# Issuing each step's up-row gathers as two groups of four, the second behind the next step's down-row gathers

## What is computed

```python
qv = (xb @ w_query).reshape(PEER_BLOCK, PEER_HEADS, 2, PEER_DHALF)
s = jnp.einsum('thsd,hskd->thsk', qv, keys)
sv, si = lax.top_k(s, PEER_TOPK)
...
g = jax.nn.softmax(fv, axis=-1)
u = expert_down[eidx]
act = jax.nn.gelu(jnp.einsum('thkd,td->thk', u, xb), approximate=False) * g
v = expert_up[eidx]
return jnp.einsum('thk,thkd->td', act, v)
```

## Time and profile before

| | us |
|---|---|
| median of 3 runs | 2114.09 (2113.5 to 2115.13) |
| the profiled execution | 2112.95 |
| its span | 2111.2 |
| PE, DVE, ACT, POOL busy | 1247.8, 1376.3, 431.7, 1052.5 |
| mean granted clock of TensorE | 0.779 |

### The profile page before, as it was taken

One profiled execution on the slowest core, in us unless ns is written; L12 is line 12 of the kernel. 1 busy time (PEld: TensorE's weight loads), 2 busy tenths in 40 slices (PEclk: granted clock), 3 DMA queues, 4 the chain that ended last, 5 costly groups with the idle time before them and its releaser, 6 DMA issues.

```text
span 2111.2 us, 20935 instructions
## 1 busy us (share of the span) xinstructions
PE 1247.8 (59%) x6676; PEld 741.8 (35%) x6676; DVE 1376.3 (65%) x3357; ACT 431.7 (20%) x920; POOL 1052.5 (50%) x1103
## 2 busy tenths in 40 slices
PE   5989899566568677777455848833224333332234
PEld 3855567453456445444223425510000000000000
DVE  3669971482477655577876676666776777777631
ACT  4112442621133221233210022211010110110000
POOL 1012220000336565566766566567767777777754
PEclk9889999687788888878778879976666665656655
DMA  9145671636669999999999999999989999999986
GB/s 297 56 159 183 204 266 55 218 100 231 227 250 373 398 402 398 394 405 396 404 404 395 402 375 398 399 386 410 409 323 409 385 409 410 410 409 409 409 341 278
DMA packets 260328, 696.11 MB, mean 330 GB/s; under 512 B 23743, under 2 KB 109847, under 8 KB 259119
## 3 DMA queue, kind: packets, MB, share of 16 engines
q0 software_dynamic: 149760, 545.33, 65.5%
q1 hardware_dynamic: 109346, 148.91, 21.0%
q10 hardware_dynamic: 1112, 0.53, 0.1%
HBM read 685.74 MB, written 9.08 MB: 329 GB/s over the span
## 4 chain that ended last, share of the span: by engine, by line
DMA 27%; POOL 17%; DVE 12%; issue 10%; PE 7%; DVEq 1%; ACT 1%; POOLq 0%; ACTq 0%
DMA arena<-in_expert_up_dram,rows 15%; DMA arena<-in_expert_down_dram,expert 11%; POOL arena L1894 9%; POOL arena L1914 8%; DVE arena L2572 6%; PE ps L2233 4%; PE ps L2265 2%; DVEq L2513 1%; DVE arena L2619 1%; PE ps L2444 1%; DMA arena<-in_expert_down_dram,sample 1%; DVE arena L2520 0%; DVE arena L2519 0%; DVE keys L2518 0%; DVE arena L2548 0%
## 5 line engine op out<-in xcount | busy, mean ns | idle before, releaser
L2572 DVE CUSTOM_DVE_ANT_0 arena<-arena,ps 128x1024 f32<-128x1024 f32 x512 | 611.5, 1218 | 283.3 <-DMA arena<-in_expert_down_dram,expert 273.0
L2233 PE MATMUL ps<-arena 128*32 128x512 f32 x2048 | 370.1, 858 | 641.5 <-DMA arena<-in_expert_up_dram,rows 641.5
L1914 POOL DMA_INDIRECT arena<-in_expert_up_dram,rows x512 | 487.3, 952 | 315.7 <-PE ps L2233 149.5
L1894 POOL DMA_INDIRECT arena<-in_expert_down_dram,expert x512 | 489.7, 956 | 231.9 <-issue 143.7
L2233 PEld LDWEIGHTS ps<-arena 128*32 128x32 f32 x2048 | 75.9, 137 | 868.2 <-issue 868.0
L2265 PE MATMUL ps<-arena 128*128 128x264 f32 (+1 forms) x1344 | 327.0, 402 | 39.6 <-ACT arena L1973 28.9
L2265 PEld LDWEIGHTS ps<-arena 128*128 128x128 f32 x1344 | 264.0, 200 | 110.8 <-ACT arena L1973 30.6
L720 PE MATMUL ps<-arena 128*128 128x256 f32 (+1 forms) x640 | 156.4, 400 | 3.5 <-ACT arena L549 3.5
L720 PEld LDWEIGHTS ps<-arena 128*128 128x128 f32 x640 | 123.6, 198 | 40.6 <-issue 19.9
L1934 ACT ACTIVATE arena<-arena 128x8 f32<-128x8 f32 x65 | 13.5, 208 | 588.5 <-DVE arena L2572 588.4
L467 POOL TENSOR_TENSOR arena<-arena 128x512 f32<-128x512 f32 x16 | 20.5, 1284 | 220.5 <-DVE arena L1073 220.5
(11 more groups left out here) (461 smaller groups left out, 1789.1 us busy)
## 6 DMA issues: line engine op xcount, KB each, us to landing
arena<-in_w_in_dram SPq DMA_DIRECT2D x42, 1024.0 KB, 17.4
arena<-in_w_ada_dram SPq DMA_DIRECT2D x32, 512.0 KB, 5.9
arena<-in_w_query_dram SPq DMA_DIRECT2D x16, 1024.0 KB, 17.2
arena<-in_w_ada_dram SPq DMA_DIRECT2D x8, 1024.0 KB, 17.5
arena<-in_w_ada_final_dram SPq DMA_DIRECT2D x16, 512.0 KB, 4.9
arena<-in_w_out_dram SPq DMA_DIRECT2D x8, 1024.0 KB, 19.3
arena<-in_expert_down_dram,expert POOLq DMA_INDIRECT x512, 12.3
arena<-in_expert_up_dram,rows POOLq DMA_INDIRECT x512, 12.3
```

The lines of the kernel that those rows point to most:

```text
L1894: G.indirect_dma_start(U[i], None, down, bass.IndirectOffsetOnAxis(ap=at, axis=0))\
L1914: G.indirect_dma_start(Vr[r][j], None, up, bass.IndirectOffsetOnAxis(ap=at, axis=0))\
L2233: last = mm(ps[32 * j:32 * j + 32, c, :], Z[:, j, m, :], Vr[r][4 * half + j][:, c * 512:(c + 1) * 512], start=(p % 4 == 0 and m == 0), sto ...
L2572: V.tensor_tensor_reduce(U[i], U[i], row, 1.0, 0.0, ALU.mult, ALU.add, dots[n % 2][:, j:j + 1]).then_inc(s_uused, 1)
```

## The change

Each step's eight up gathers are issued in two groups of four. The loop over the steps now issues: down of step n, the last four of up step n-5, the first four of up step n-4. Before it issued: down of step n, all eight of up step n-4. The gathers are the same, their buffers, semaphores and waits too; only their order in POOL's queue differs. PE's, DVE's, ACT's and SP's programs do not change.

```diff
-            def gather_up(n):
+            def gather_up(n, some=range(VR)):
...
-                if g != S and g % 4 == 0:
+                if some[0] == 0 and g != S and g % 4 == 0:
                     pool.wait_ge(s_idxT, g // 4 + 1)
...
-                if r and V_before[n] is None:
+                if some[0] == 0 and r and V_before[n] is None:
...
-                for j in range(VR):
+                for j in some:
...
-            for n in range(NSTEP):
+            first4, last4 = range(0, 4), range(4, VR)
+            for n in range(NSTEP - 1):
                 gather_down(n)
-                for m in at_step.get(n, ()):
-                    gather_up(m)
+                if n > LAG:
+                    gather_up(n - LAG - 1, last4)
+                if n >= LAG:
+                    gather_up(n - LAG, first4)
+            gather_down(NSTEP - 1)
+            gather_up(NSTEP - 2 - LAG, last4)
+            for m in at_step[NSTEP - 1]:
+                gather_up(m)
```

## The result

| | before | changed |
|---|---|---|
| median, us | 2114.35 (2113.5 to 2115.13, 4 runs) | 2138.54 (2135.67 to 2145.83, 4 runs) |
| ratio | | 1.0121, interval 1.0101 to 1.0141 |
| the profiled execution, us | 2112.95 | 2145.83 |
| its span, us | 2111.2 | 2144.1 |
| PE, DVE, ACT, POOL busy, us | 1247.8, 1376.3, 431.7, 1052.5 | 1253.9, 1363.7, 431.2, 1054.6 |

The changed kernel is 24.2 us slower (1.2%). The forecast was 17 us slower. In the changed kernel the lines behind the edit have numbers higher by 7: `add` is L2240, DVE's products L2579, the end of `topk` L2569, the turning of indices L2221 and DVE's copy of them L2782.

A forecast was written before the change was run, and what follows sets the result against it. The prediction took DMA's gather stream to bound the kernel, with POOL ahead by the cushion. Terms 13.8 + 1.0 - 2.2 + 4.4 = 17.0 us gave a median of 2131 us, 0.8% slower; range 2109 to 2152, the forecast case's own 2119 to 2146.

The forecast's parts named there:

- cushion: How late POOL may issue gathers before DMA has nothing to do, under the late work: 13.0 - 6.05 = 6.9 us.
- Terms 1 and 2: Units 7 and 9: late PE work delays DVE, then POOL; gaps 6.8 and 4.8 us, plus 1.5 and 2.6 in units 8, 10.
- In the other units with late work: Late-work units besides 7 to 10: POOL would be late by less than the cushion, so priced at nothing.
- The rebuilding of the cushion between units: Between late-work units POOL catches up, issuing in 1.24 us against 1.48 per gather: 3.8 us a step, 7.6 a unit.
- The 12% taken off for weights: In the gaps of units 7 to 10 SP's weight loads can use the engines, cutting 15.7 to 13.8 us.
- Term 3: At the samples, where POOL waits for topk: a later half delays add, ACT's softmax and DVE, +1.0 us.
- Term 4: Gap at 1640 us: the samples' two adds, set apart by 12 gathers, no longer hold POOL up twice, -2.2 us.
- Term 5: Behind the last down rows: a second POOL wait for add follows the first with an empty queue, +4.4 us.
- That the cushion absorbs all: Rival for units 7 to 10: only terms 3 to 5 count, 2117 us, no change; chance 24%.
- That gaps close: Rival: gaps at 1220, 1370 and 1640 us close, gaining 7.6 us, 2106.5 or 2111 us; chance 14%.
- DVE as the bound of the four units: Rival for units 7 to 10: cushion not rebuilt between units, 46 us in all, 2160 us; chance 10%.

The follow-up runs named there:

- the ring exchanged: Kernel before, whole groups, only the buffer places of the last four steps' up rows exchanged: 2219.99 us, ratio 1.0008, and 2219.21 us, ratio 1.0011 on the third chip.

## Why the prediction was right, and where its sizes were not

**The mechanism was right.** The forecast was that POOL's down gathers come to wait for DVE, DVE for PE's late work, and PE for the late half, and that DMA pays what goes beyond its cushion. The windows, the waits and the instructions in unit 7 show each link. The run with PE's order changed takes out the middle link, and 19 of 23.4 us under the late work go with it (by the medians of the whole program, 15.1 of 24.2).

**Cushion.** Issue to landing, by the median, fell from 13.0 us to 9.0 us for up rows in the same 200 us, and the shortest took 5.1 instead of 8.6. So the lead was really used up there. Line of the changed kernel, up rows from 900 to 1100 us:

```profile
DMA to landing us min/median/max: 5.1/9.0/19.0
```

The size of 6.9 us is less sure than the prediction made it. The row of 6.05 us is the fourth gather behind the wait with the queue drained. The first one, issued at 2047.95, took 4.4 us in the kernel before (and the one at 2073.51 took 4.2 in the changed kernel):

```profile
DMA to landing us min/median/max: 4.4/4.4/4.4
```

Taken from that row the cushion is 13.0 - 4.4 = 8.6 us, and the forecast's own latenesses give 5.1, 0, 3.1 and 0.9 us for units 7 to 10, 9.1 in all. No run tells the two sizes apart.

**Terms 1 and 2, units 7 to 10.** At 400 GB/s as full speed, the windows lose 10 x (1 - 231/400) + 10 x (1 - 327/400) = 4.2 + 1.8 = 6.0 us in unit 7 (forecast 6.8), 30 x (1 - 340/400) = 4.5 in unit 8 (1.5), and 10 x (1 - 319/400) = 2.0 at 1010 us in unit 9. With the window ahead of that one (373 GB/s, 0.7 us) unit 9 has 2.7 (4.8), and unit 10, with 330 GB/s at 1050 us, has 1.8 (2.6). The sum is 15.0 against 15.7. The sum agrees, but in part by luck: unit 8 got 3.0 us too little and unit 9 2.1 too much, and with a cushion of 8.6 us the same reading would have given 9.1. Unit 8's reading was taken over from unit 9's pattern, without the instructions' own places.

**The step that was mis-sized** is the sentence "In the other units with late work DVE has more room before POOL needs it, and I price them at nothing". The loss up to step 40 is 23.4 us, not 13.8. At the start, 670 to 710 us, the window loses 40 x (1 - 336/400) = 6.4 us, and with the first groups whole this gap is not there. Later the gaps of 3.2 us at 1220 and 2.2 us at 1370 us have gone, and three have come, at 1210, 1240 and 1260 us: 10 x (1 - 320/400) = 2.0, 10 x (1 - 255/400) = 3.6 and 10 x (1 - 309/400) = 2.3, on balance 2.5 us more. The windows so give 6.4 + 15.0 + 2.5 = 23.9 us, where DVE's clock has 23.4. The four units had been chosen because DVE's place ahead of POOL could be read there; the others were not found clear, but left unread. The rebuilding of the cushion between units (7.6 us a unit) had been worked out for one stretch and held for all. The 12% taken off for weights gave 13.8; the sum of 15.0 lies between that and 15.7.

How large the mis-sizing is depends on the execution. The kernel split in the late steps only has the same order up to there and lost 17.3 - 3.7 + 5.1 = 18.7 us up to step 34, the changed kernel 24.2 - 6.2 + 5.1 = 23.1. Two executions of one order so differ by 4.4 us here. By the medians the whole change costs 24.2 us.

**Term 3, the samples**, +1.0 us: right. DVE goes on and POOL follows, in the changed kernel:

```profile
1565.18 0.17 DVE L2562 RECIPROCAL arena<-arena 128x1 f32<-128x1 f32 x1 [1.01 <-ACT arena L1936]
...
1566.64 0.94 POOL L1894 DMA_INDIRECT arena<-in_expert_down_dram,expert  x1 [13.92 <-DVE expert L2569]
```

POOL's wait is 13.92 us where it was 12.96, 0.96 more, and DVE's clock gives +0.9 from step 40 to 41. It gives +1.0, +0.9 and +0.7 in the other three kernels of the first chip that are split there, and 0.0 in the one whose groups are whole there again.

**Term 4, the gap at the samples' `add`s**, -2.2 us: the cause went, the gain did not come. POOL's waits for them got shorter, 1.25 and 2.18 us, together 3.4, where the kernel before has 3.79 and 2.20, and from 1640 to 1690 us the rate stays at 408 to 410 GB/s, as forecast. But the clock of DVE shows +0.2 us from step 41 to step 64, and +0.7 and +1.3 in the two others that are split there. A little later, at 1692 us, POOL waits 2.49 us for `topk`, and that is where the hole now is (324 GB/s from 1690 to 1700 us, 2.1 us). One gap closed and another of the same size opened a little behind it, where the kernel before has none.

**Term 5, the end**, +4.4 us: right up to PE's last `add`. The two waits are there:

```profile
2073.51 0.94 POOL L1914 DMA_INDIRECT arena<-in_expert_up_dram,rows  x1 [10.79 <-PE ps L2240]
...
2088.35 0.94 POOL L1914 DMA_INDIRECT arena<-in_expert_up_dram,rows  x1 [5.18 <-PE ps L2240]
```

10.79 and 5.18 us, where 10.7 and 4.4 were forecast. Yet the end moved by 2.2 us only. The last `add` of the program says where the rest went, first in the kernel before, then in the changed one:

```profile
2094.55 3.64 PE L2233 MATMUL ps<-arena 128*32 128x512 f32 x16 [2.10 <-DMA arena<-in_expert_up_dram,rows]
```

```profile
2129.22 1.92 PE L2240 MATMUL ps<-arena 128*32 128x512 f32 x16 [1.69 <-DMA arena<-in_expert_up_dram,rows]
```

It starts 65.2 us behind DVE's step 64 in one and 74.3 us behind it in the other, 9.1 us more. Less the 5.1 us of four gathers that is 4.0 us, near the forecast. But it runs at a granted clock of 0.50 (1.2 GHz) in the kernel before and of 1.00 (2.4 GHz) in the changed one, and so takes 1.92 instead of 3.64 us; 13.0 us follow behind it in both. These 1.7 us, and not a wait that is cheaper than its length, make the difference. In the changed kernel the last five `add`s, each alone behind a wait of 1.7 to 3.2 us, take 1.92, 3.38, 1.92, 3.38 and 1.92 us in turn, so which length the last one has was not foreseeable. In the kernel with the first groups whole the last one takes 3.21 us, and the end moved by 90.8 - 81.9 - 5.1 = 3.8 us.

By the fit that the Trainium skill gives ("DMA: Bandwidth & Descriptors", section "Anatomy of one DMA — SWDGE (gpsimd) path") the second wait would have been 1.6 us; the trace has 5.18, and the measurement decides.

**What no term had**: 6.2 us ahead of the stage. Nothing was changed there, and all five profiled executions on the first chip that are not of the kernel before begin the stage 2.9 to 7.0 us later than its one. By ACT's instructions this gathers below 300 us. It looks like the spread of executions: on the slower chips the profiled executions begin the stage at 556.8 to 565.1 us (559.8 in the kernel before on the first chip), and the changed kernel itself at 566.0 on the first chip and at 556.8 on the third. It was not tested by itself. It is not in the forecast's mechanism and may be part of the 7 us by which the forecast was short.

**The rivals.** That the cushion absorbs all is refuted by the windows. That gaps close: the one at 1370 us did, the others moved. DVE as the bound of the four units (46 us) is refuted on the first chip, since their sum is 15.0 us. On the third chip, though, the same kernel loses 47.7 us.

## What to carry to other kernels

When gathers are moved in a queue, ask whose work is queued behind the wait for them on the engine that reads them, not only whether the queue's own distances stay. The distance of POOL from one half to the same half of the next step stayed here, and 24 us were lost, some 15 of them since PE's hand-written order put unrelated work behind the delayed `add`. The lead of the queue, issue to landing under load less issue to landing when drained (13.0 less 4.4 to 6.05 us here), is the measure of how late the issuing engine may be. It is shared by everything that can be late in that stretch, so every unit has to be read, not the ones with the clearest pattern. A split order also has a seam: where it meets whole groups again, it costs a wait by itself (4.5 us by DVE's clock here).

And a gap that is filled where it stood need not come off the time. Leaving the first groups whole filled one of some 6 us, and the median fell by 1.4 us (5.5 by the ratios, whose intervals overlap).

## What the runs showed of the hardware that was not expected

The second and third chips are some 5% slower, for the kernel before (2219.56 and 2215.39 against 2113.97 us) and, on the third, for the changed one (2263.05 against 2138.54 us). The gathers themselves are not slower when they run: from 1780 to 1800 us the rate is 409 and 410 GB/s in the two kernels with the ring exchanged, as in the kernel before on its chip. It is the mean from 1700 to 1900 us that is lower, 362 GB/s instead of 410. What differs is idle time of engines that nothing in the profile explains. On DVE it is spread over many instructions. The same group on the page, first of the kernel before on its chip, then of the kernel with the ring exchanged on the third chip:

```profile
L2520 DVE MAX8 arena<-arena 128x8 f32<-128x128 f32 (+1 forms) x99 | 33.5, 339 | 7.6 <-issue 0.4
```

```profile
L2520 DVE MAX8 arena<-arena 128x8 f32<-128x128 f32 (+1 forms) x99 | 33.5, 339 | 38.3 <-issue 32.4
```

The busy time is the same, 33.5 us, and the idle time ahead of it that the profile can put down to nothing grew from 0.4 to 32.4 us. Over DVE's whole program from 1400 us on it is 62.7 us in 46 pieces of up to 5.8, where the kernel before on the first chip has 1.4 in 4. What holds DVE up was not found.

On that chip the change costs 47.7 us instead of 24.2, the opposite of what was expected (1.008) from the slower gathers. One reading is that DVE's unexplained pauses use the same cushion that the change uses, so that both together exceed it more often. It fits the longer waits of POOL for DVE (15.74 us, the longest in the changed kernel on the first chip being 12.8), but no run tested it.
